# A decoder layer on one core: the A heads' values by seven block products, with the sums of x on GpSimd

## What is computed

```
h = rmsnorm(x, attn_norm[l])
proj = jnp.einsum('bsd,de->bse', h, w_in[l])
...
va = proj[..., c1:c2].reshape(b, s_len, N_HEADS_A, HEAD_DIM).transpose(0, 2, 1, 3)
```

## Time and profile before

| | |
|---|---|
| median of 3 runs | 1989.87 us (1989.74 to 1991.38) |
| the profiled execution | 1990.41 us |
| its span, first to last instruction | 1988.6 us |
| TensorE busy | 1978.7 us |
| VectorE busy | 1597.8 us |
| ScalarE busy | 1096.9 us |
| GpSimd busy | 140.6 us |

### The profile page before, as it was taken

The page is one execution under the profiler, slowest core; times in us unless marked ns, Lnnn a source line. Parts: engine busy times, 40 slices in busy tenths (PEclk is TensorE's granted clock), DMA queues, the critical chain, the costliest instruction groups (busy, mean ns, idle before and its releaser), DMA issues.

```text
span 1988.6 us, 29175 instructions
## 1 busy us (share of the span) xinstructions
PE 1978.7 (100%) x10348; PEld 1701.3 (86%) x10348; DVE 1597.8 (80%) x2311; ACT 1096.9 (55%) x2009; POOL 140.6 (7%) x241
## 2 busy tenths in 40 slices
PE   9999999999999999999999999999999999999998
PEld 8888888888888998888888888888888888888886
DVE  5326777777776899999999999999998688697886
ACT  6326666666436655545555555645556355566643
POOL 1002223332100000000000000000000000000000
PEclk9999999999999999999999999999999999999999
DMA  8332222223434343434443433433336946546433
GB/s 301 96 96 75 70 69 70 70 70 92 145 98 153 123 138 138 136 129 138 138 136 130 137 138 127 145 131 138 134 134 228 313 123 215 179 150 223 125 129 133
DMA packets 131913, 274.07 MB, mean 138 GB/s; under 512 B 13568, under 2 KB 13600, under 8 KB 130768
## 3 DMA queue, kind: packets, MB, share of 16 engines
q1 hardware_dynamic: 119344, 233.36, 36.5%
q0 software_dynamic: 6640, 23.82, 3.1%
q10 hardware_dynamic: 5808, 15.23, 2.1%
HBM read 240.89 MB, written 31.46 MB: 137 GB/s over the span
## 4 chain that ended last, share of the span: by engine, by line
PE 99%; issue 0%; DMA 0%; DVE 0%; ACT 0%; SPq 0%; POOLq 0%; POOL 0%
PE bank L730 27%; PE bank L733 14%; PE bank L657 9%; PE bank L659 9%; PE bank L658 9%; PE bank L599 6%; PE bank L601 6%; PE bank L600 6%; PE bank L789 3%; PE bank L788 3%; PE bank L787 3%; PE bank L814 2%; PE bank L799 1%; PE bank L831 1%; PE bank L798 1%; PE bank L830 1%
## 5 line engine op out<-in xcount | busy, mean ns | idle before, releaser
L730 PE MATMUL bank<-s_two,t_hi 128*128 128x512 f32 x2352 | 557.3, 390 | 0.0
L730 PEld LDWEIGHTS bank<-s_two,t_hi 128*128 128x128 f32 x2352 | 433.5, 188 | 84.7
L1288 ACT ACTIVATE t_hi<-t_raw 128x1792 fp32r<-128x1792 f32 x176 | 302.5, 1720 | 358.4 <-DVE t_raw L1875 269.7
L1881 DVE TENSOR_TENSOR t_lo<-t_raw,t_hi 128x1792 fp32r<-128x1792 f32 x176 | 355.3, 2019 | 21.0 <-ACT t_hi L1288 21.0
L1021 ACT ACTIVATE w_hi<-raw 128x512 fp32r<-128x512 f32 x300 | 188.4, 629 | 273.0 <-PE bank L659 200.3
L1581 DVE TENSOR_TENSOR w_lo<-raw,w_hi 128x512 fp32r<-128x512 f32 x300 | 205.6, 687 | 143.2 <-ACT w_hi L1021 142.4
L733 PEld LDWEIGHTS bank<-s_two,t_lo 128*128 128x128 f32 x2352 | 298.8, 191 | 10.0 <-DVE t_lo L1881 0.2
L733 PE MATMUL bank<-s_two,t_lo 128*128 128x256 f32 x2352 | 302.1, 283 | 0.0
L1872 DVE TENSOR_TENSOR t_raw<-t_raw 128x1024 f32<-128x1024 f32 x176 | 214.7, 1220 | 16.1 <-DMA t_raw<-in_w_gu 14.0
L599 PE MATMUL bank<-h_hi,w_hi 128*128 128x512 f32 x416 | 165.9, 399 | 1.0 <-DVE h_lo L1585 1.0
L601 PE MATMUL bank<-h_lo,w_hi 128*128 128x512 f32 x416 | 162.7, 391 | 0.0
(11 more groups left out here) (223 smaller groups left out, 3310.1 us busy)
## 6 DMA issues: line engine op xcount, KB each, us to landing
t_raw<-in_w_gu SPq DMA_DIRECT2D x348, 256.0 KB, 2.8
raw<-in_w_down SPq DMA_DIRECT2D x112, 256.0 KB, 3.6
raw<-in_w_in SPq DMA_DIRECT2D x104, 256.0 KB, 2.7
gu_mid<-part POOLq DMA_DIRECT2D x43, 512.0 KB, 2.9
gu_next<-gu_mid SPq DMA_DIRECT2D x36, 512.0 KB, 6.3
raw<-in_w_out SPq DMA_DIRECT2D x64, 256.0 KB, 2.9
fast_y<-in_w_down SPq DMA_DIRECT2D x24, 512.0 KB, 4.5
raw<-in_w_v SPq DMA_DIRECT2D x32, 256.0 KB, 2.6
```

The lines of the kernel that those rows point to most:

```text
L730: mm = nc.tensor.matmul(b[:, :], t_hi[r][:, ti, q, :], both, start=d == 0 and q == 0, stop=d == DOUBLES - 1 and q == 1 and i < 4, skip_gro ...
L1288: nc.scalar.activation(t_hi[r][:, :, :, :].rearrange("p a q c -> p (a q c)"), t_raw[r][:, 1:8, :, :].rearrange("p a q c -> p (a q c)"), AC ...
L1881: nc.vector.tensor_tensor(t_lo[r][:, :, :, :].rearrange("p a q c -> p (a q c)"), t_raw[r][:, 1:8, :, :].rearrange("p a q c -> p (a q c)"), ...
```

## The change

The product for V is cut into halves in three ways: tokens (half 0 and 1), features of x (near, slices 0 to 7, and far, 8 to 15) and columns (1 and 2). The eight products of halves become seven, each of four units of 12 matmuls: V1 is near(0) by W11; V5 is near(1)+far(1) by W12-W11; V6 is far(1)+near(1)-near(0) by W22-W12+W11; V7 is near(0)-near(1) by W22-W12; V3 is far(0) less V6's sum of x, by W22; V2 is far(0) by W21; V4 is far(1) by the V6 weights less W21. Each runs in two banks. Products that are parts of several results are copied out (`v_keep`), copied back in ahead of the next product (`v_seed`), or added by VectorE in the bank (`v_add`).

VectorE makes the differences of weights (`v_sum`), GpSimd first scales `x_first` by the gains in place and then makes the sums of x (`x_sums`). Both kinds are split into halves by `vf_high`, `vf_low`, `vx_high`, `vx_low`, with four buffers for half units of weights and two for sums of x. V's weights no longer pass the ring `raw`, but come in pieces of 256 x 512 into eleven buffers of their own (`v_x`, `v_y`, `v_z`). The order of TensorE is `EARLY`: four V units, then the first pair's 12 units (P) alternating with 12 V units (S), then 12 V units. The four memsets of `k_lo` move from VectorE to GpSimd; the constants' loads are split in two parts on GpSimd's queue; row 3 of x is loaded after row 2's square, and row 2 after row 0's. A single matmul into bank 6 (`bank_whole`) is added.

```diff
+V1, V5, V6, V7, V3, V2, V4 = range(7)
+V_UNITS = 28
+V_BANK = ((0, 4), (5, 7), (6, 1), (0, 4), (6, 1), (5, 7), (0, 4))
+BANK_Q0 = 1
+EARLY = tuple(("S", j) for j in range(4)) + sum(((("P", i), ("S", 4 + i)) for i in range(12)), ()) + tuple(("S", j) for j in range(16, 28))
...
+        load_v(v_y[0], raw_vy[0], 1, 1, 0)
+        load_v(v_y[1], raw_vy[1], 1, 1, 1)
+        load_v(v_x[0], raw_vx[0], 1, 2, 0)
+        load_v(v_y[2], raw_vy[2], 1, 1, 2)
+        load_v(v_z[1], raw_vz[1], 1, 1, 3)
+        load_v(v_x[1], raw_vx[1], 1, 2, 1)
+        load_unit_in(8)
+        load_unit_in(9)
+        load_v(v_x[2], raw_vx[2], 1, 2, 2)
+        load_unit_in(10)
+        load_unit_in(11)
+        load_v(v_z[0], raw_vz[0], 2, 2, 0)
+        sp.wait_ge(sq_done, 2)
+        load_v(v_x[3], raw_vx[3], 1, 2, 3)
+        sp.wait_ge(v_sum_done, v_sum_count(4))
+        load_v(v_y[0], raw_vy[0], 1, 2, 0)
+        sp.wait_ge(v_sum_done, v_sum_count(5))
+        load_v(v_y[1], raw_vy[1], 1, 2, 1)
+        load_unit_in(12)
+        sp.wait_ge(v_sum_done, v_sum_count(6))
+        load_v(v_y[2], raw_vy[2], 1, 2, 2)
+        load_unit_in(13)
+        sp.wait_ge(v_sum_done, v_sum_count(7))
...
-        def v_unit(n, k):
...
-            for t in range(NT):
-                mm = wide_products(t, bank[BANK_VA[n][t]], h_hi[:, k, :], h_lo[:, k, :], k, unit % 4, k == 0, k == KD - 1)
...
+        def v_unit(j):
+
+            p, u = j // 4, j % 4
+            if u == 0 and p in (V6, V7, V2, V4):
+                pe.wait_ge(v_moved, {V6: 4, V7: 8, V2: 10, V4: 12}[p])
+            if u == 0 and p == V3:
+                pe.wait_ge(v_added, 3)
+            if V5 <= p <= V3:
+                pe.wait_ge(vx_lo_done, j - 3)
+            for i in range(2):
+                q = (2 * j + i) % 4
+                pe.wait_ge(vf_lo_done, 2 * j + i + 1)
+                for tp in range(2):
+                    if V5 <= p <= V3:
+                        ah, al = vx_hi[j % 2][:, i, P * tp:P * (tp + 1)], vx_lo[j % 2][:, i, P * tp:P * (tp + 1)]
+                    else:
+                        k, t = 2 * u + i + (0 if p == V1 else 8), tp + (2 if p == V4 else 0)
+                        ah, al = h_hi[:, k, P * t:P * (t + 1)], h_lo[:, k, P * t:P * (t + 1)]
+                    mm = three(bank[V_BANK[p][tp]][:, :], ah, al, vf_hi[q][:, :], vf_lo[q][:, :],
+                               p in (V1, V5) and u == 0 and i == 0, u == 3 and i == 1)
+                mm.then_inc(vf_used, 1)
...
+            for e, (kind, j) in enumerate(EARLY):
+                if kind == "S":
+                    v_unit(j)
+                else:
+                    if j == 4:
+                        pe.wait_ge(acc_taken, 1)
+                    if j == 8:
+                        pe.wait_ge(acc_taken, 3)
+                        pe.wait_ge(vb_all_done, 1)
+                    tall_unit(U_FIRST // 4 + j // 4, j % 4, (BANK_Q0, BANK_KB, BANK_VB)[j // 4], h_hi, h_lo)
+                if e == 9:
                     pe.wait_ge(ident_loaded, 16)
-                    spread_r(squares[:, :].rearrange("p (t c) -> p t c", c=P), 1, BANK_PT)
-                if k == 8:
-                    pe.wait_ge(acc_taken, 2)
+                    spread_r(o_low[:, :].rearrange("p (t c) -> p t c", c=P), 1, BANK_Q)
+                if e == 11:
+                    pe.wait_ge(rbc_done, 1)
+                    nc.tensor.matmul(bank[BANK_Q][:, :], h_hi[:, 0, 0:P], h_hi[:, 0, :], start=True, stop=True,
+                                     skip_group_check=True).then_inc(bank_whole, 1)
...
+            if h >= 4:
+                act.wait_ge(vf_used, h - 3)
+            nc.scalar.activation(vf_hi[h % 4][:, :], v_source(j)[:, i, :], ACT.Copy).then_inc(vf_hi_done, 1)
...
+        def v_seed(p):
+
+            if p == V6:
+                act.wait_ge(v_moved, 2)
+                act.wait_ge(bank_whole, 1)
+                act.wait_ge(acc_taken, 2)
+            if p == V7:
+                act.wait_ge(vf_used, 24)
+            if p == V2:
+                act.wait_ge(v_taken, 2)
+            if p == V4:
+                act.wait_ge(v_added, 5)
+            for tp in range(2):
+                src = {V6: v_kept1[:, tp, :], V7: bank[V_BANK[V6][tp]][:, :], V2: v_kept1[:, tp, :], V4: bank[V_BANK[V7][tp]][:, :]}[p]
+                nc.scalar.activation(bank[V_BANK[p][tp]][:, :], src, ACT.Copy, scale=-1.0 if p == V4 else 1.0).then_inc(v_moved, 1)
...
+            for e, (kind, j) in enumerate(EARLY):
+                if kind == "P":
+                    split(*ahead_of(U_FIRST + j))
+                else:
+                    if V5 <= (j + 1) // 4 <= V3:
+                        vx_high(j + 1)
+                    for h in (2 * j + 3, 2 * j + 4):
+                        if h < 2 * V_UNITS:
+                            vf_high(h)
+                if e < 3:
+                    split(*ahead_of(U_FIRST + e - 3))
+                if e == 0:
+                    square_row(1)
+                if e == 2:
+                    square_row(2)
+                    load_row(3)
+                if e == 6:
                     square_row(3)
-                if s == 10:
-                    kb_high(0)
-                    vb_high(0)
-                if s == 16:
-                    v_take(0)
-                if s == 21:
-                    q_high("A", proj[0], 3, qa_hi_done)
-                if s in (25, 26):
-                    k_high(4, s == 26)
...
+                if e == 12:
+                    v_seed(V6)
...
+                if e == 31:
+                    v_seed(V2)
+                if e == 32:
+                    v_take(V3, 1, 0)
+                if e == 33:
+                    v_seed(V4)
...
+        def v_sum(j):
+
+            p, u = j // 4, j % 4
+            x, z = v_x[u][:, :, :].rearrange("p k c -> p (k c)"), v_z[u][:, :, :].rearrange("p k c -> p (k c)")
+            if p == V5:
+                y, loaded = v_first(u)
+                dve.wait_ge(raw_vx[u], 16)
+                dve.wait_ge(loaded, 16)
+                nc.vector.tensor_tensor(x, x, y[:, :, :].rearrange("p k c -> p (k c)"), ALU.subtract).then_inc(v_sum_done, 1)
+            elif p == V6:
+                dve.wait_ge(raw_vz[u], z_count(u, 1))
...
+        pool.wait_ge(xt_lo_done, KD)
+        for u in range(4):
+            for k in (2 * u, 2 * u + 1, 2 * u + 8, 2 * u + 9):
+                nc.gpsimd.tensor_scalar(x_first[:, k, :], x_first[:, k, :], gains[:, G_ATTN + k:G_ATTN + k + 1], 1.0,
+                                        ALU.mult, ALU.mult).then_inc(x_gained, 1)
+            pool.wait_ge(x_gained, 4 * u + 4)
+            x_sums(4 * V5 + u)
+        nc.gpsimd.dma_start(ident[:, :], c_ident).then_inc(ident_loaded, 16)
+        for dst, src in ((band, c_band), (slope, c_slope), (sink, sinks[0, :].partition_broadcast(P))):
+            nc.gpsimd.dma_start(dst[:, :], src).then_inc(consts_loaded, 16)
+        invert(1, slice(0, NT))
+        for p in (V6, V7, V3):
+            for u in range(4):
+                x_sums(4 * p + u)
```

More of the change, by code:

```diff
@@ L463, in _, with load_unit_in, load_v @@
-        load_v(1)
-        for p in range(1, PAIRS):
-            load_pair(p)
+        def load_unit_in(unit):
+            p = 0 if unit < U_PAIR else 1 + (unit - U_PAIR) // PAIR_U
+            c, j = (unit - u_pair(p)) // 4, unit % 4
+            load(unit // 4, j, tall(col_in(("q", "k", "qb")[c], p), j))
+        def load_v(dst, loaded, rows, n, u):
+            row = 1024 * (rows - 1) + 256 * u
+            sp.dma_start(dst[:, :, :], w_v[row:row + 256, 512 * (n - 1):512 * n].rearrange("(k p) c -> p k c", p=P)).then_inc(loaded, 16)
@@ L466, in _ @@
+        load_v(v_z[3], raw_vz[3], 2, 2, 3)
+        for unit in range(14, 23):
+            load_unit_in(unit)
+        sp.wait_ge(vf_lo_done, 26)
+        load_v(v_y[0], raw_vy[0], 1, 2, 3)
+        for unit in range(23, 27):
+            load_unit_in(unit)
+        for u in range(4):
+            sp.wait_ge(vf_lo_done, 34 + 2 * u)
+            load_v(v_z[u], raw_vz[u], 2, 1, u)
+        for unit in range(27, U_OUT):
+            load_unit_in(unit)
         with sp.Fori(0, 2) as g:
@@ new lines, in v_take @@
+        def v_take(p, n, half):
+            if p == V5:
+                act.wait_ge(v_added, 5)
+                act.wait_ge(vx_lo_done, 12)
+            else:
+                act.wait_ge(vf_used, 8 * (p + 1))
+            for tp in range(2):
+                t = tp + 2 * half
+                nc.scalar.activation(o_t[:, 4 * n:4 * n + 4, P * t:P * (t + 1)], bank[V_BANK[p][tp]][:, :].rearrange("p (a c) -> p a c", c=P),
+                                     ACT.Copy, scale=(neg_inv if p == V4 else inv)[:, t:t + 1]).then_inc(v_taken, 1)
@@ L1243, in _ @@
             elif what == "l":
[L1244 removed]
+                load_row(m)
+            elif what == "f":
+                vf_high(m)
             elif what == "r":
@@ new lines, in v_add @@
+        def v_add(p, q):
+            for tp in range(2):
```

(19 more changed lines are left out.)

310 lines of the change are left out of this document (198 added, 112 removed).

## The result

The changed kernel takes 1999.71 us (median of 5 runs, 1998.86 to 2004.15), the kernel before in the same session 1990.24 (1989.74 to 1991.38). The ratio is 1.005, with a 95% interval of 1.0038 to 1.0061: 9.5 us slower, where 4.5 us faster was forecast, and outside the range of 1980.8 to 1991.5. The profiled execution took 2000.4 us, its span is 1998.5.

What follows compares the result with a forecast made beforehand. TensorE, almost never waiting, was taken as the bound. 10.66 us of products saved, less waits of 2.6, 1.2, 1.4 and 0.6 and 0.4 for shared reads, gave -4.5: 1985.4 us against the median 1989.87; range 1980.8 to 1991.5.

Steps and rivals of the forecast that it cites:

- What bounds the kernel: Whole run: TensorE busy 1978.7 of 1988.6 us, so a product removed is time won and each TensorE wait is lost.
- what a product costs: V products, by distance of starts: 0.2268 us each, 2.72 us for a unit of 12.
- the gain: V's products fall from 384 to 336, saving 10.89 us; one added product leaves 10.66 us net.
- the shared reads: GpSimd's scalings and sums against VectorE: 1.3 us in the second wait, 0.4 in the first; ends nothing and 15.6.
- The 1.82 us tick: Earlier trace from 207.09 us: a 0.19 us GpSimd tick lasts 1.82 while VectorE runs operations with two SBUF inputs.
- The rival that did this: GpSimd's 12 sums get in ahead of VectorE, 58 to 80 us, costing it 15.6 us: 1996, chance 0.12.
- First wait: Head's loads: unit 8's late landing delays V's weight halves on ScalarE; 2.2 us near 36 us, then 0.4.
- Second wait: Turned 1/rms, at the transposes near 59 us: row 3, means, power and widening come late, 1.2 us.
- Third wait: V6's seeds before S8, near 69 us: ScalarE's two seeds wait for VectorE's last take, 1.4 us.
- Fourth wait: V2's seeds at S20: they stand on ScalarE behind a high half waiting for S19's first half, 0.6 us.
- The clock: Rival: clock falls in the 2.2 us gap, 0.5 per us at 1.2 GHz, five us +2.5: 1988, chance 0.05.
- Costed at nothing: V's larger loads after 50 us, SP's order, adds and takes, pair 1's ScalarE work: covered by slack, no cost.

Runs made afterwards that it cites:

- tiny scalings: GpSimd's 16 scalings and four first sums on one column, against the kernel with VectorE's sums, three order edits and S4's splits moved forward: 1981.15 us.
- tiny sums: GpSimd's twelve later sums of x made on one column of each slice only, against the change: 1986.84 us.
- with the order of the engines mended: Halves of S1 to S3, row 3 and seeds moved earlier: on the change 1989.45 us, on the kernel whose sums VectorE makes 1982.38.
- the spread kernel: The change with GpSimd's sums not back to back: three before the power, one after the widening, the rest one per V unit: 1990.59 us.
- squares behind: Halves of S1 to S3 put ahead of rows 0 and 1's squares and unit 8, on the kernel whose sums VectorE makes: 1986.93 us.
- VectorE's sums: The change with VectorE making the twelve later sums of x, one per V unit from S4 to S15, GpSimd none of them: 1988.35 us.

## Why the prediction was wrong

**What bounds the kernel; what a product costs; the gain: right.** Starts are 0.227 us apart in the new profile too, and the kernel with nearly all waits gone (tiny scalings) is 9.9 us faster than before, where 10.66 us net were counted.

**The step that failed: the shared reads.** The sum has 1.3 us for GpSimd's twelve later sums (one sum ahead of the widening) and 0.4 for its scalings. That term was mis-sized: without the twelve sums' reads the change is 12.9 us faster (tiny sums), and with the order of the engines mended they still cost 6 to 7 (1989.45 against 1982.38). VectorE lost 10.6 us between 60.7 and 81.8, where the ends given were nothing and 15.6. The prediction took the low end, "because behind a busy VectorE it was GpSimd that stood still". The 1.82 us tick of the earlier trace rows shows that this happens, and so do the sums of 3.94 and 4.02 us. But it is the exception: ten of the twelve spread-out sums got in behind at most one VectorE operation, and in the change and in the spread kernel alike a sum cost VectorE 0.8 to 0.9 us. That is the other row, a `w_lo` of 1.04 under a GpSimd sum, and it should have been priced once for each sum. The rival that did this said 1996 at a chance of 0.12. Its point of decision, 8 us lost beyond the slack, was not reached by its own count: 10.6 less some 4 of cover is 6.6, about what the sums cost once the order is mended. The time went past 1996 all the same. In the change the longer waits met a late order, and the lower clock came on top. Without the sums the forecast would have been about 1985.4 - 1.3 = 1984.1, and tiny sums measured 1986.84; of the 2.7 us between, the fall of the clock at 39 us in its profile is 1.6. Of the 14.5 us between the forecast for the profiled execution (1985.9) and its 2000.4, 8.5 are waits ahead of pair 1 (14.7 for 6.2), 3.9 the lower clock, 1.5 waits in the later stages; 0.6 stay open.

**First wait: 2.6 us forecast, 4.1 measured.** Place and cause were right (the order on ScalarE, as squares behind shows). Unit 8's copy began at 35.51, for a landing at 34.3 in my count. Missed were 0.99 us before it, since row 0's square stands ahead of S1's second half in the same way, and 0.76 behind it, where 0.4 was forecast.

**Second wait: 1.2 forecast, 2.85 measured.** Row 3's bytes ended before 50 us, as forecast (49.7). But "copy and square end at 52.3" took unit 12's weights to be there; they came at 52.3, so the square ended at 54.8 and the means came at 58.7, not 56.3. Then the widening took 3.46 in place of 0.9. TensorE, itself 2 us later than I had it, hid part.

**Third wait: 1.4 forecast, 6.0 measured**, the shut-out again: with tiny sums it is 0.6, with VectorE's sums 1.7. **Fourth wait: 0.6 forecast, 0.43 measured**, at the place named and gone once the seeds are moved.

**The clock: 0.05 was too little.** It fell with each of the two gaps over 2.8 us, and that cost 3.9 us; with the 2.35 us gap at 39 us, the one that the rival named, it did not (behind the same gap it did in four of the six experiments that have it). The price was right (0.5 per us at the lower level), but it is no rival by itself: it comes on top of long waits.

**Costed at nothing**: V's takes, adds and keeps and the loads after 50 us; no wait is seen there. What I had not counted are 0.5 to 1.5 us of waits in the gate/up and down stages, in every changed kernel's profile and not in the one of before. Their cause was not tried.

## What to carry to other kernels

GpSimd is no free hand beside a VectorE whose operations read two SBUF tensors: price each GpSimd operation that reads SBUF as a loss on VectorE (0.8 to 0.9 us for a sum of 1.3 here, in a row or alone), or let VectorE do it itself (0.6 us here), unless VectorE works from banks at the time or GpSimd only writes. When a change takes products away from a TensorE that never waited, look at each engine's order for a copy that stands behind something late: moving three such places gave 6.0 us here; with VectorE's sums alone only 1.6 of the products' 10.7 us had shown. And a gap of TensorE of 2 us or more costs more than its length: 11 of the 14 seen here brought 1.1 to 2.1 us of lower clock as well.
